# Expert down weights read as pairs of rows, with gate and up weight columns taken two apart to match

## What is computed

```python
def expert_choice(h, w_router, w_gate, w_up, w_down):
    B, T, D = h.shape
    C = EC_FACTOR * T // N_EXPERTS
    aff = jax.nn.softmax(jnp.einsum('btd,de->bte', h, w_router).astype(jnp.float32), axis=-1)
    gsel, idx = lax.top_k(aff.transpose(0, 2, 1), C)
    xs = jax.vmap(lambda hb, ib: hb[ib])(h, idx)
    hid = jax.nn.silu(jnp.einsum('becd,edf->becf', xs, w_gate)) * jnp.einsum('becd,edf->becf', xs, w_up)
    ye = jnp.einsum('becf,efd->becd', hid, w_down) * gsel[..., None].astype(h.dtype)
    return jax.vmap(lambda yb, ib: jnp.zeros((T, D), yb.dtype).at[ib.reshape(-1)].add(yb.reshape(-1, D)))(ye, idx)
```

## Time and profile before

| what | us |
|---|---|
| median of 3 runs | 1805.66 |
| lowest and highest of them | 1805.21, 1807.56 |
| the profiled execution's own time (its span) | 1807.7 |
| PE busy within it | 1619.1 |
| PE's weight loads busy | 1281.1 |

### The profile page before, as it was taken

The page is one execution under the profiler, slowest core; times in us unless marked ns, Lnnn a source line. Parts: engine busy times, 40 slices in busy tenths (PEclk is TensorE's granted clock), DMA queues, the critical chain, the costliest instruction groups (busy, mean ns, idle before and its releaser), DMA issues. The chain is left out here.

```text
span 1807.7 us, 69734 instructions
## 1 busy us (share of the span) xinstructions
PE 1619.1 (90%) x27905; PEld 1281.1 (71%) x27905; DVE 829.0 (46%) x2593; ACT 572.2 (32%) x2228; POOL 391.3 (22%) x2166
## 2 busy tenths in 40 slices
PE   6999988986999999888869999899599998998885
PEld 3554457446999989888735554664389988998885
DVE  2299768262333323232245996943623232423233
ACT  2200245235545432211130003542355554221211
POOL 1100000002343424332310000000124333333332
PEclk9999999997999999999989999999799999999998
DMA  9356640237999999999953412221599999999992
GB/s 348 129 184 235 233 174 1 105 127 284 402 409 409 409 409 409 409 409 409 361 206 140 157 58 102 108 94 35 202 374 409 409 409 409 408 409 409 409 407 111
DMA packets 146722, 502.59 MB, mean 278 GB/s; under 512 B 6217, under 2 KB 6642, under 8 KB 146578
## 3 DMA queue, kind: packets, MB, share of 16 engines
q1 hardware_dynamic: 142288, 488.96, 69.5%
q0 software_dynamic: 3264, 10.88, 1.8%
q10 hardware_dynamic: 1026, 1.25, 0.2%
HBM read 494.76 MB, written 6.31 MB: 277 GB/s over the span
## 5 line engine op out<-in xcount | busy, mean ns | idle before, releaser
L950 PE MATMUL ps<-v_sb,weight_ring 128*64 128x80 f32 x16384 | 589.3, 234 | 51.7 <-DMA weight_ring<-in_w_gate_dram 20.8
L950 PEld LDWEIGHTS ps<-v_sb,weight_ring 128*64 128x64 f32 x16384 | 577.3, 138 | 63.0 <-DMA weight_ring<-in_w_gate_dram 25.0
L967 PE MATMUL ps<-v_sb,weight_ring 128*64 128x80 f32 x8192 | 296.7, 234 | 31.7 <-DVE v_sb L1693 19.9
L967 PEld LDWEIGHTS ps<-v_sb,weight_ring 128*64 128x64 f32 x8192 | 288.4, 138 | 40.0 <-DVE v_sb L1693 25.0
L705 PE MATMUL ps<-mix,weight_ring 128*128 128x128 f32 (+1 forms) x976 | 271.0, 439 | 2.1 <-ACT mix L1054 1.2
L1238 ACT ACTIVATE v_sb<-mix 128x8 f32 x1520 | 185.5, 205 | 223.6 <-PE ps L950 146.1
L1719 DVE TENSOR_TENSOR qk<-qk,v_sb 128x8 f32 x1520 | 212.3, 194 | 90.8 <-issue 90.0
L1848 POOL COPY v_sb<-mix 128x8 f32 x1040 | 145.2, 198 | 479.0 <-PE ps L950 417.7
L1861 POOL TENSOR_TENSOR qk<-qk,v_sb 128x8 f32 x1040 | 198.7, 232 | 181.7 <-DVE v_sb L1708 178.5
L705 PEld LDWEIGHTS ps<-mix,weight_ring 128*128 128x128 f32 x976 | 148.1, 194 | 122.8 <-issue 119.8
L1443 DVE SCALAR_TENSOR_TENSOR weight_ring<-u_gate,conv_cols,weight_ring 128x655 f32<-128x655 f32 x240 | 195.3, 899 | 0.0
(11 more groups left out here) (195 smaller groups left out, 1240.5 us busy)
## 6 DMA issues: line engine op xcount, KB each, us to landing
weight_ring<-in_w_down_dram SPq DMA_DIRECT2D x64, 2048.0 KB, 23.7
weight_ring<-in_w_gate_dram SPq DMA_DIRECT2D x48, 2048.0 KB, 20.9
weight_ring<-in_w_up_dram SPq DMA_DIRECT2D x48, 2048.0 KB, 23.6
weight_ring<-in_w_mod_dram SPq DMA_DIRECT2D x24, 2048.0 KB, 9.0
weight_ring<-in_w_in_dram SPq DMA_DIRECT2D x10, 2048.0 KB, 8.3
spare<-in_w_gate_dram SPq DMA_DIRECT2D x32, 512.0 KB, 10.4
weight_ring<-in_w_out_dram SPq DMA_DIRECT2D x4, 2048.0 KB, 9.4
rope_sb<-in_w_gate_dram SPq DMA_DIRECT2D x16, 512.0 KB, 11.3
```

Of the source, the lines that this page charges most:

```text
L950: last = nc.tensor.matmul(ps[c * HALF:(c + 1) * HALF, 2 * (i % 2) + f // BLK, f % BLK * CAP:(f % BLK + 1) * CAP], w[:, kk, o:o + HALF], pi ...
L967: last = nc.tensor.matmul(ps[c * HALF:(c + 1) * HALF, 4 + d // BLK, d % BLK * CAP:(d % BLK + 1) * CAP], w[:, kk, o:o + HALF], hid[:, k, :] ...
```

## The change

`expert_src` gives another view of `w_down`: partition p of chunk q holds rows 256q+2p and 256q+2p+1, which lie next to each other in DRAM, and next to each other in the slot as well. A down unit is two such chunks, so it is 256 pieces of 8 KB where it was 512 of 4 KB. Its slot, bytes, waits and place in SP's order are the same.

Piece k of the slot now holds, on partition m, row 256(k//2) + 2m + k%2. `hid` must have its values in that order, so block f of the gate and up products takes the weight columns 256(f//2) + f%2 + 2m: the 64 columns of one weight load lie 8 bytes apart in the slot and span 508 bytes, where they were adjacent and spanned 256. The gate and up units are loaded as before, in rows of 4 KB. `down` is unchanged in the code, and its weight columns are adjacent.

```diff
+PAIR = 2
...
             def expert_src(l, e, i):
-                w, half = (w_gate, w_up)[i % 2] if i < 4 else w_down, i // 2 if i < 4 else i - 4
+                if i >= 4:
+                    return w_down[l, e].rearrange("(q p j) n -> p q (j n)", p=P, j=PAIR)[:, 2 * (i - 4):2 * (i - 3), :]
+                w, half = (w_gate, w_up)[i % 2], i // 2
                 return w[l, e].rearrange("(k p) n -> p k n", p=P)[:, half * 4:half * 4 + 4, :]
...
             def expert_unit(l, e, i):
-                sp.dma_start(ring[:, UNIT_SLOTS[l][i], :].rearrange("p (k n) -> p k n", k=KD // 2), expert_src(l, e, i))\
-                  .then_inc(expert_loaded[i].sem, 16)
+                sp.dma_start(ring[:, UNIT_SLOTS[l][i], :].rearrange("p (k n) -> p k n", k=KD // 2 if i < 4 else KD // 4),
+                             expert_src(l, e, i)).then_inc(expert_loaded[i].sem, 16)
...
                             for kk in range(KD // 2):
                                 k = (i // 2) * (KD // 2) + kk
                                 for c in range(2):
-                                    o = f * P + c * HALF
+                                    o = f // PAIR * PAIR * P + f % PAIR + PAIR * c * HALF
                                     last = nc.tensor.matmul(
                                         ps[c * HALF:(c + 1) * HALF, 2 * (i % 2) + f // BLK,
                                            f % BLK * CAP:(f % BLK + 1) * CAP],
-                                        w[:, kk, o:o + HALF], picked_t[:, k, :],
+                                        w[:, kk, o:o + PAIR * HALF - 1:PAIR], picked_t[:, k, :],
                                         start=(k == 0 and f % BLK == 0), stop=(k == KD - 1 and f % BLK == BLK - 1))
```

## The result

| | before | changed |
|---|---|---|
| median of 5 runs, us | 1807.56 | 1799.55 |
| lowest to highest, us | 1805.21 to 1809.41 | 1796.52 to 1803.27 |
| span of the profiled execution, us | 1807.7 | 1798.6 |

The ratio on record is 0.995 with a 95% interval of 0.9936 to 0.9963: 9.0 us less on 1807.56, between 6.7 and 11.6. The two medians as such lie 8.0 us apart. The forecast was 8.5 less.

What follows compares the result with a forecast made beforehand. Weight transfers in both layers' experts were taken as the bound, with PE having room. Larger down pieces save 8.5 us, the strided load costs 0: 1805.66 - 8.5 = 1797.2 us on the median, range 1788 to 1807.

Steps and rivals of the forecast that it cites:

- What bounds: Both layers' experts: transfers set the time, 30.8 us an expert against PE's 27.6; PE has 46.1 us of waits as room.
- Part 1: Down units in 8 KB pieces: 9.2 ns a piece beyond its bytes, 0.147 us a unit, 58 units, 8.5 us less.
- One piece, not two: SP's queue: an 8 KB run passes whole, inferred from 5,120 B runs; packets fall from 142,288 to 125,904.
- Part 2: Gate and up weight loads with columns 8 bytes apart: taken as 0 us, at most 295 us of PE time.
- rival 2: Gate and up: the strided weight load binds PE, 295 us more work, time about 2055 us; chance 0.12.
- The point from which rival 2 decides: Gate and up stretch per expert: 17.93 us may grow to 19.1 before the time changes; rival 2 decides from 19.5.
- room equals the waits of the groups: PE in the experts: its room is its 46.1 us of weight waits, 37.6 us after the 8.5 gained.
- PE's wait: PE's wait for gate, up and down weights: 46.1 us less 8.5, about 38 us after the change.
- the rate of 413 GB/s: Full slices of the experts: 12.58 MB in 30.5 us, 413 GB/s after the change, 409 before.
- The transfers' pace: Experts' weight transfers: six units, 12.58 MB at 409 GB/s, take 30.8 us an expert; down landings lay 31.3 us apart.
- one engine that lags the other fifteen: End of layer 1: at 34 GB/s one of 16 engines lags and PE sees its landings; the saving is unchanged.
- One sign: End of layer 1: down landings still 31.3 us apart, not about 31.0, would show the forecast wrong.

## Why the prediction was right

- **What bounds.** Shown: a slower PE costs nothing until some 50 us of work have been added, and the rate of the transfers sets the time in four sizes of piece, both ways.
- **Part 1, 9.2 ns a piece.** Shown, by size at 2, 8 and 16 KB. The 8.5 us came as 9.0, with 7.4 where only the pieces were changed. That they meet within 0.5 us is luck: the interval is 6.7 to 11.6, and the price of a piece is known no better than to 1 or 2 ns in 9. The estimate from the Trainium skill, "DMA: Bandwidth & Descriptors" (section "Why small descriptors are slow (HBM only)"), 3.3 us, lies outside the measured 6.7 to 11.6; the runs side with the trace.
- **One piece, not two.** The packet count showed it, for 16 KB too.
- **Part 2, zero.** Shown by the stride alone, 1.0004, and by the pieces alone. The rule of the Trainium skill, "SBUF — State Buffer" (section "Door 1: The DMA port swizzle"), two hits in a 16-byte line, lets 8 bytes pass, and the runs agree that nothing shows at 8 bytes (17.93 us) while 12 bytes cost (22.44). They don't show an edge between the two, since at 8 bytes a load can hide under the 70.0 ns of a pair. From 12 to 16 bytes the cost grows on, so there is no second fixed rate.
- **The point from which rival 2 decides** was wrong: I had 19.1 us an expert for the first loss and 19.5 for a visible loss against the kernel before, from the sum of PE's waits. At 19.55 nothing shows. By the nominal room of 60 us the first loss comes at 17.93 + 60/32 = 19.8, and a time 3.6 us over the kernel before, which needs 60 + 9.0 + 3.6 us more, at 20.2. The step that failed is "room equals the waits of the groups": pauses also leave tails in the busy sum. Its price was mis-sized as well: I took 106 ns a pair for a load at half rate, as a least, and one 16 bytes apart gives 120.9.
- **PE's wait** of 38 us came as 39.4, and the rate of 413 GB/s as 411 to 414.
- **The transfers' pace was read too short.** I had 30.8 us an expert from the mean rate and called landings 31.3 apart an agreement. Between the second up units it is 31.64, and in the changed kernel 31.33 where the rate gives 30.5. So 0.8 us an expert are in neither sum; as it is the same on both sides, it doesn't enter the gain. The prediction's one engine that lags the other fifteen would make such a difference, but no run here separates the engines, and this stays open.
- **One sign was badly chosen.** I wrote that down landings 31.3 us apart at the end of layer 1 would speak against the forecast. The 31.3 was the last distance alone, and in the changed kernel the chain passes up landings there and not down landings:

```profile
1701.26 25.09 DMA weight_ring<-in_w_up_dram
...
1732.27 25.36 DMA weight_ring<-in_w_up_dram
```

These landed at 1726.35 and 1757.63, again 31.3 us apart, which says nothing, since other units are compared with each other. The same unit over several experts is a good sign: 31.64 fell to 31.33 in layer 0, and the last five steps of layer 1 went from 31.45 to 31.14 in the mean. At the very end only 41 GB/s flow (1760 to 1770 in the window above), the share of one or two of the sixteen engines; why they lag no run here tests.

## What to carry to other kernels

Where transfers are full, divide two full stretches with different run lengths into a cost per byte and a cost per piece; here that gave a forecast well inside the interval of the measurement, and it held from 2 to 16 KB. Rows can be made neighbours on a partition if the producer of the other operand takes its columns in the same order; here the weight loads hid columns two float32 apart behind the products, and three apart no longer. An engine's room before it binds can be more than its waits add up to: test it by adding known work, or count a tail for each wait. To see a change of 1% in a pace, take the same unit over several rounds.

## What was not expected of the hardware

- Float32 weight loads of 64 columns, two halves at a time beside products of 80 columns: 8 bytes apart 70.0 ns a pair (as with adjacent columns), 12 bytes 87.7, 16 bytes 120.9.
- 8.0 to 9.7 ns per contiguous run on each DMA engine (intervals from 5.3 to 12.5), whatever its length from 2 to 16 KB, and 421 GB/s when the runs are 8 KB.
- 64 transfers more, of 1 MB each instead of 2 MB, cost nothing behind a full queue.
